# RWKV branch: the transposes inside the block inverse on VectorE (32x32 blocks) instead of TensorE products with the identity

## What is computed

```python
def step(s, inp):
    r_t, w_t, k_t, v_t, kk_t, a_t = inp
    sa = jnp.einsum('bhvk,bhk->bhv', s, -kk_t)
    s = s * w_t[:, :, None, :] + sa[..., None] * (kk_t * a_t)[:, :, None, :] + v_t[..., None] * k_t[:, :, None, :]
    return s, (jnp.einsum('bhvk,bhk->bhv', s, r_t) if with_output else None)
```

## Time and profile before

| | |
|---|---|
| time, median of 3 runs | 5019.98 us |
| the profiled execution, its span | 5020.2 us |
| TensorE (PE) busy in the span | 4595.0 us, 92% |
| VectorE (DVE) busy in the span | 2086.9 us, 42% |
| ScalarE (ACT) busy in the span | 1338.8 us, 27% |
| GpSimd (POOL) busy in the span | 431.0 us, 9% |
| the RWKV part | 52.0 to 1203.6 us of the span |

### The profile page before, as it was taken

The page is one execution under the profiler, slowest core; times in us unless marked ns, Lnnn a source line. Parts: engine busy times, 40 slices in busy tenths (PEclk is TensorE's granted clock), DMA queues, the critical chain, the costliest instruction groups (busy, mean ns, idle before and its releaser), DMA issues.

```text
span 5020.2 us, 85352 instructions
## 1 busy us (share of the span) xinstructions
PE 4595.0 (92%) x36404; PEld 2831.8 (56%) x36404; DVE 2086.9 (42%) x3869; ACT 1338.8 (27%) x2490; POOL 431.0 (9%) x385
## 2 busy tenths in 40 slices
PE   6899889988998899979998999989999999989999
PEld 3566666666555554464443544444787544444787
DVE  2555555453355542130112337463343237463343
ACT  2334333332222211010001124341232124341232
POOL 0121111110222230000000000020000000020000
PEclk8999999988999999989999999999999999999999
DMA  5200000000111024238998211113220211113221
GB/s 227 74 29 19 5 19 19 2 26 13 42 47 38 34 91 186 97 128 353 399 408 353 86 56 55 45 67 138 104 101 34 101 63 47 45 63 139 106 101 51
DMA packets 76819, 503.34 MB, mean 100 GB/s; under 512 B 9480, under 2 KB 10008, under 8 KB 34328
## 3 DMA queue, kind: packets, MB, share of 16 engines
q1 hardware_dynamic: 76440, 497.88, 25.9%
HBM read 472.66 MB, written 25.19 MB: 99 GB/s over the span
## 4 chain that ended last, share of the span: by engine, by line
PE 79%; DVE 8%; issue 6%; DMA 2%; ACT 2%; POOL 1%; SPq 0%; PEldq 0%; PEld 0%; DVEq 0%; ACTq 0%; POOLq 0%
PE ps L228 76%; PE ps L231 3%; DMA upper<-in_ew 2%; DVE upper L263 2%; ACT upper L286 2%; DVE upper L247 1%; DVE upper L239 1%; POOL upper L3461 1%; DVE upper L255 1%; DVE lower L239 1%; DVE upper L243 1%; ACT lower L286 0%; DVE lower L247 0%; DVE lower L243 0%; DMA lower<-in_ada 0%
## 5 line engine op out<-in xcount | busy, mean ns | idle before, releaser
L228 PE MATMUL ps<-lower 128*128 128x512 f32 (+12 forms) x7024 | 1919.4, 440 | 67.2 <-issue 22.8
L228 PEld LDWEIGHTS ps<-lower 128*128 128x128 f32 (+3 forms) x7024 | 952.1, 186 | 777.6 <-issue 602.8
L228 PE MATMUL ps<-upper 64*64 64x64 f32 (+8 forms) x15584 | 836.4, 259 | 145.2 <-DVE upper L263 38.7
L286 ACT ACTIVATE upper<-ps 128x512 f32<-128x512 f32 (+5 forms) x967 | 446.9, 491 | 1757.9 <-PE ps L228 1284.3
L228 PEld LDWEIGHTS ps<-upper 64*64 64x64 f32 (+4 forms) x15584 | 595.8, 144 | 453.8 <-issue 216.2
L228 PE MATMUL ps<-lower,upper 64*64 64x64 f32 (+6 forms) x7504 | 714.4, 313 | 51.7 <-DMA lower<-in_ada 20.9
L228 PE MATMUL ps<-rounded 128*128 128x512 f32 x3072 | 711.0, 394 | 7.5 <-DVEq L213 7.5
L228 PEld LDWEIGHTS ps<-rounded 128*128 128x128 f32 x3072 | 578.6, 188 | 139.1 <-issue 8.3
L228 PEld LDWEIGHTS ps<-lower,upper 64*64 64x64 f32 (+3 forms) x7504 | 381.2, 144 | 334.3 <-issue 264.4
L286 ACT ACTIVATE upper<-upper 128x512 f32<-128x512 f32 (+9 forms) x709 | 364.7, 523 | 723.7 <-DVE upper L259 186.1
L228 PE MATMUL ps<-upper,lower 128*128 128x512 f32 (+4 forms) x1584 | 485.8, 477 | 8.1 <-DVE lower L247 1.8
(11 more groups left out here) (82 smaller groups left out, 2130.2 us busy)
## 6 DMA issues: line engine op xcount, KB each, us to landing
lower<-in_ew SPq DMA_DIRECT2D x140, 1024.0 KB, 10.3
upper<-in_ew SPq DMA_DIRECT2D x52, 1024.0 KB, 12.8
lower<-in_b0f SPq DMA_DIRECT2D x16, 2048.0 KB, 8.0
lower<-in_b1f SPq DMA_DIRECT2D x16, 2048.0 KB, 8.0
upper<-in_ada SPq DMA_DIRECT2D x18, 1024.0 KB, 5.4
lower<-in_wrkv SPq DMA_DIRECT2D x8, 1728.0 KB, 7.1
lower<-in_b0g SPq DMA_DIRECT2D x8, 1536.0 KB, 6.5
gad<-upper SPq DMA_DIRECT2D x48, 256.0 KB, 2.0
```

Source lines behind the costliest of these rows:

```text
L228: return self.e.matmul(out, lhsT, rhs, start=start, stop=stop)
L286: self.e.activation(out, in_, func, bias=bias, scale=scale, accum_out=accum).then_inc(line.up(*event), 1)
```

## The change

TensorE's "level" step keeps the 8 products with `N`, now side by side in 128 columns of each bank, and drops the 8 with the identity. VectorE gets a "level" step of 4 transposes per lane and level: each takes 64 partitions x 128 elements of `X` (one half e, one head, both chunks) and writes them, transposed in blocks of 32x32, into `PX`, to partitions 0 to 63 or 64 to 127 by the head. ScalarE's copy shrinks to 128x256. "merge" on TensorE waits for both. As each helper does, a transpose waits for the lane's own last VectorE instruction.

```diff
+    def turn(self, line, out, a, *event):
+        self.wait_ge(line)
+        self.e.transpose(out, a).then_inc(line.up(*event), 1)
...
             for u in range(2):
                 for e, hd in four:
                     r = heads[e]
-                    pe.mm(ps[heads[hd], e, 128 * u:128 * u + 64], N(u, hd)[r, r], x(hd, u)[r, :], True, True)
-                for e, hd in four:
-                    r = heads[e]
-                    last = pe.mm(ps[heads[hd], e, 128 * u + 64:128 * u + 128], x(hd, u)[r, :], I[e], True, True)
+                    last = pe.mm(ps[heads[hd], e, 64 * u:64 * u + 64], N(u, hd)[r, r], x(hd, u)[r, :], True, True)
             last.then_inc(team.pe.up(*use), 1)
             banks.give(use, team.act, *use)
         elif name == "merge":
             lev, = z
             ps = v3(banks.take(use, 2), 512)
             pe.wait_ge(team.act, "level", j, d, p, lev)
+            pe.wait_ge(team.dve, "turned", j, d, p, lev)
...
+        elif name == "level":
+            lev, = z
+            PX, halves = b.PX[d].rearrange("p (e u c) -> p e u c", e=2, u=2), (slice(0, 64), slice(64, 128))
+            for e in range(2):
+                for hd in range(2):
+                    v.turn(team.dve, PX[halves[hd], e, :, 64:128], v3(X[halves[e], hd, :], 64),
+                           *(("turned", j, d, p, lev) if e and hd else ()))
...
-        if name in ("tri", "products", "merge", "corner"):
+        if name in ("tri", "products", "level", "merge", "corner"):
...
-            a.copy(team.act, v3(b.PX[d], 256), v3(k.pair(use), 512)[:, :, 0:256], *use)
+            a.copy(team.act, b.PX[d].rearrange("p (e u c) -> p e u c", e=2, u=2)[:, :, :, 0:64],
+                   v3(k.pair(use), 512)[:, :, 0:128].rearrange("p e (u c) -> p e u c", u=2), *use)
```

## The result

The changed kernel takes 5106.57 us (median of 4 runs, 5104.8 to 5107.95) against 5020.4 us (4 runs). The ratio is 1.0171 (95% interval 1.0157 to 1.0186): 86 us slower. The forecast was 58 us slower; its likeliest case ran from 5035 to 5130.

What follows compares the result with a forecast made beforehand. TensorE was taken to set the pace, with VectorE's free time perhaps in the wrong places: 90 + 9 + 5 + 10 = 114 us lost, 56 gained, so 5020 + 58 = 5078 us, range 5005 to 5145.

Steps and rivals of the forecast that it cites:

- likeliest case: Whole kernel: VectorE's transposes come late and TensorE waits; 5035 to 5130 us, chance 0.65.
- The price of a transpose: VectorE, each level: 960 added transposes at an estimated pitch of 0.33 us, 317 us in all.
- Where the loss is: RWKV part: 58 us longer, all others unchanged; TensorE's waits up by 110 us, nearly all at transposes before merges.
- the removal: TensorE, 240 levels: 16 identity records fewer per level, 0.234 us each level, 56 us gained.
- the shortfalls: Merges waiting for late transposes: 11.3 us per middle block, 90 us over eight blocks, before smaller additions.
- the same seven pairs: Block 3's level pairs with too little VectorE idle time before the pick: 0.6 to 3.5 us lost each.
- the eight pairs: Block 3's other level pairs, of 15, with idle of about 3.2 us and more or other steps between: nothing lost.
- The clock: TensorE in the RWKV part: granted clock 0.93 may fall when it idles more; unpriced, left in the range.
- The place in VectorE's queue: Where VectorE has no idle left before a pick, the pick and next level are late too: 10 us.
- TensorE is relieved and VectorE keeps up: Rival: delayed merges only eat idle time that came anyway; up to 56 us gained, 4964 to 5005 us, chance 0.14.
- Half rate: Rival: float32 transposes at a pitch of about 0.48 us; 5174 us, chance 0.11 for 5130 and more.
- cancelling: Rival: pitch 0.25 us or lower, or losses overlapping idle time; 5010 to 5030 us, chance 0.10.

Runs made afterwards that it cites:

- the run with both: Changed kernel with the 1920 products with the identity kept on TensorE, written to PSUM columns nobody reads: 5113.43 us, ratio 1.0179 to the kernel before.
- the 84 chosen levels: Changed kernel with transposes only at 84 levels where VectorE had idled long enough, the other 156 as before the change: ratio 0.999 to the kernel before.
- the removal alone: Changed kernel without the transposes as well as the products with the identity, merges reading zeros: 4991.76 us, ratio 0.9934 to the kernel before.
- short fillings: 2 to 8 constant products in TensorE's waits, read by nobody: on the kernel before 5009.23 us (ratio 0.9976), on the changed kernel 5100.12 us (1.0158).
- the long filling: Kernel before with constant products in TensorE's waits, read by nobody, 16 of them in front of a join: ratio 1.0021 to the kernel before.

## Why the prediction was right, and where it was off

**The price of a transpose** was right: 304 ns and a pitch of 0.33 us, which was the estimate. The Trainium skill, page VectorE: DVE Perf Modes, section The three transpose paths, has 311 ns for a larger tile of 2-byte elements, which lies beside it. By the Trainium skill, same page, section Rules for kernel authors, VectorE's transpose is the fastest within a bank. Here this misleads, as the prediction said: TensorE's small products flow at 15 ns a record, and even a single record of one lasts 226 ns against 304.

**Where the loss is** was right: all of it in the RWKV part, 83.5 us of it at the merges, and the two pairs shown lose 3.0 and 1.6 us for a forecast of 3.5 and 2.0. TensorE's idle time grew by 81 us, the prediction said 110 to 114; its busy time grew by 6 us, the prediction had it fall by some 50. The two misses, 33 us too much and 62 too little against the sum of 114 and 56, go opposite ways, so that +58 came as near to +86 as it did is in part luck.

**The term that was wrong is the removal**, "56 us gained". It was 16 records x 0.0146 us x 240, TensorE's stream taken at full value and set against the shortfalls. Measured, the removal is worth 33 us alone and 4 us (with some 13 of uncertainty) beside the transposes. Forecast: 114 lost, 56 gained, +58. Measured: 90 lost, 4 gained, +86. The shortfalls of the prediction had been reckoned with a TensorE that arrives 0.47 us earlier; without the removal the same seven pairs give 7 x 0.47 x 8 = 26 us less, 88 us, close to the 90 of the run with both. So the additive sum was right for what was added and wrong for what was removed: in the eight pairs that were to keep their 0.47 us, TensorE gets to the next wait earlier and waits there. The windows show it: from the run with both to the changed kernel TensorE's busy time in the part falls by 45 us (1074.5 to 1029.4), and its idle time rises by 31 (177.5 to 208.8).

**The clock** was left in the range without a price. It fell from 0.93 to 0.88, and the same work then takes longer; with the ends of matmuls exposed at the waits, that is how TensorE's busy time rose while its records fell. How much is which was not measured. Raised by filling, it gave 6 us, which the intervals do not tell from nothing, with fillings that may have cost something themselves. That most of the busy time it added would otherwise have been waiting is an inference.

**The place in VectorE's queue** was put at 10 us ("the pick itself and the next level are late too"). With the wait taken away, and the products kept, it is 68 us: the same delay shows up at the merge when TensorE waits there, and at the next level when it does not. As shares of one delay the two numbers of the forecast, 104 at the merges and 10 at the picks, could not be read off one at a time.

**The rivals.** "TensorE is relieved and VectorE keeps up" holds only for the 84 chosen levels, and even there without a measurable gain. Half rate and cancelling fell with the 304 ns.

What stays open: how the 33 us of the removal alone fall short of 56, split between clock and waits; what the lower clock costs the changed kernel, apart from what the fillings cost; and whether the 84 levels together with short fillings would beat 5009 us, which was not tried.

## What to carry to other kernels

Work moved to a half-idle engine is free only in idle time that ends with someone else's result and is longer than the work; read the idle time in front of each instruction that follows, not the busy share, and count whatever stands behind in the same queue. Don't book the relief of the first engine at full value in the same sum: once it waits for the second, what it saves turns into more waiting. Where TensorE does set the pace, constants multiplied in its waits and sized to them raised its clock and brought 0.24% here; twice as long they cost 0.21%.

## What the hardware showed unexpectedly

- Filling raised the granted clock of the part from 0.93 to 0.97 in the kernel before and from 0.88 to 0.95 in the changed one, with nothing real altered.
- A 128x128x128 float32 product in a row of its kind takes 0.23 us, two records that begin 0.11 apart (20 records, first row, of the long filling). That is about a quarter of a 128x512 one, whose two records begin 0.43 us apart or more (8 records, second row, of the kernel before behind the RWKV part).

```profile
595.20 2.50 PE L228 MATMUL ps<-lower 128*128 128x128 f32 x20
...
4311.79 3.70 PE L228 MATMUL ps<-lower 128*128 128x512 f32 x8
```

  The weight loads of the ten small products also follow one another without a gap:

```profile
595.20 2.31 PEld L228 LDWEIGHTS ps<-lower 128*128 128x128 f32 x20
...
L228 PEld LDWEIGHTS ps<-lower 128*128 128x128 f32 x20 | 2.3, 192 | 0.1
```

  The Trainium skill, page TensorE: Matmul & The Clock Gate, section LDWEIGHTS, gives columns / 1.2 ns, an estimate of 107 ns for 128 columns. The trace has one load every 116 ns (2.31 us for 20), and 192 ns for a single record. Whether the loads or the products set the pace of such a row, no run here shows.
- VectorE's transposes of 64 partitions x 128 elements keep their 304 ns whether they cross from one half of the partitions to the other (305 and 306 ns on average) or not (298 and 308), and do not overlap even when nothing makes them wait.
